# A convolution's magnitude sums on VectorE, a router that picks the first expert's rows itself, and two attentions in one stage

## The chip, the core and the metric

The kernel is one program on one core of a Trainium2 chip. It holds two transformer blocks in fp32. The metric is the device time of the whole program in microseconds (us); lower is better. The engines are named as in the profile: PE (TensorE matmul), PEld (its weight load), DVE (VectorE), ACT (ScalarE), POOL (GpSimd), SP (SyncE, which here only issues DMAs).

## The reference, cut to what matters

Three parts of the reference are touched. The first is the long convolution of the first block; o runs over its two orders:

```python
taps = jnp.concatenate([fwd, jnp.zeros_like(fwd[:1]), jnp.flip(bwd[1:], axis=0)], axis=0)
taps = taps / (jnp.sum(jnp.abs(taps), axis=0, keepdims=True) + EPS)
return jnp.fft.rfft(taps, axis=0)
...
for o, gate in enumerate((x1, x2)):
    zf = jnp.fft.rfft(z, n=2 * n, axis=1)
    conv = jnp.fft.irfft(zf * filt[None, :, o], n=2 * n, axis=1)[:, :n]
    z = gate * (conv + skip[o] * z)
```

The second is the mixture of 16 experts (4 groups of 4, the best two experts of one group for each of 512 tokens):

```python
scores = jax.nn.sigmoid((ht @ router_w).astype(f32))
sel = scores + router_b.astype(f32)
group_score = lax.top_k(sel.reshape(-1, N_GROUPS, EXPERTS_PER_GROUP), TOP_K)[0].sum(-1)
group = jnp.argmax(group_score, axis=-1)
_, idx = lax.top_k(jnp.where(in_group, sel, -jnp.inf), TOP_K)
for e in range(N_EXPERTS):
    hid = jax.nn.silu(ht @ w_gate[e]) * (ht @ w_up[e])
    out = out + gates[:, e:e + 1] * (hid @ w_down[e])
```

The third is two attentions of the second block that don't depend on one another. The dilated one has three groups of four heads (head size 64) that are merged by a softmax over their log-sums; the memory one has four heads (size 128) of 512 queries against 256 memory rows:

```python
alpha = jax.nn.softmax(jnp.stack(lses, axis=0), axis=0)
o_dil = jnp.sum(alpha[..., None] * jnp.stack(outs, axis=0), axis=0)
...
sm = jnp.einsum('bqhc,bkhc->bhqk', qm, kv[:, :, 0]) * (MEM_HEAD_DIM ** -0.5)
pm = jax.nn.softmax(sm, axis=-1)
om = jnp.einsum('bhqk,bkhc->bqhc', pm, kv[:, :, 1]).reshape(B, S, MEM_WIDTH)
```

## The kernel before, in words

The program is a row of stages. Each is one `nc.Block()`, in which every engine has its own written-out list of instructions, and semaphores order them across engines; all engines meet at the end of a stage. PSUM has 8 banks of 128x512, `K.ps`. A matmul whose operands are plain fp32 stands in the profile as two records. The large weight products are written as three matmuls with operands split into a rounded high part and a rest: ACT makes the high part of a weight chunk (`high`), DVE or POOL subtracts to get the low part (`low`).

Weights come through a ring (`Ring`, L49) of four slots of 1 MB. SP issues load k once `used` has reached k - 3, and that count grows when a chunk's slot has been read; in the expert stage DVE's `low` does it.

**Long convolution** (`hyena_stage`, L1671). For each order o, four token phases i: PE makes the filter values (`filters`), ACT the decay window, DVE multiplies them and makes the sum and difference (`tap_pair`), ACT takes their magnitudes (`magnitude`), and PE adds the magnitudes up over the tokens by multiplying with ones (`sums`, L1735, two matmuls for each of the four phases). DVE adds the skip term to the first row (`patch`). PE transforms signal (`"z"`) and filter (`"f"`), each in two halves j of four groups D, B, A, C (`group`, two matmuls of 128x512 each). ACT evicts D and B, DVE adds and subtracts A and C (`add`). DVE multiplies the spectra (`products`, seven operations of up to 128x2048), corrects one row (`row_products`, `row_again`), and PE transforms back (`inverse`) into the four banks `B_OUT`, from where DVE multiplies with the gate. The banks `B_OUT` are those of D, B, A and C, and so `inverse` waits until `add` of the last filter half has read them.

**Router** (`router_stage`, L2272). ACT and DVE finish the norm, PE multiplies with the router's matrix and transposes the hidden tokens into rows `K.h_rows`. DVE ranks the 4 groups and the 4 experts in each group by pairwise comparisons, one after another, each waiting for the one before (`then`, `tt`, L2378). `masked` lets PE count each token's place in its expert's list. From the places DVE works out the slot numbers (`K.put`, `keyed`), and POOL scatters the token rows into `h_slots` in DRAM with eight indirect DMAs. Behind that DVE makes the weights, the overflow list, the rates of the later recurrence (`le` to `K.lru_rate`) and the norm of the memory rows (`m_rec`, `m_root`, eight scalings of `K.memT`). SP stores `gate_rows` and waits until they have landed.

**Experts** (`moe_stage`, L2485). For expert e, SP reads its 128 rows from `h_slots`, PE transposes them (`turn_rows`), ACT and DVE split them (`high_rows`, `low_rows`), and PE multiplies with six weight chunks: `hidden(e)` takes four, `down(e)` two, each chunk 12 matmuls of 128x512. Parts of four chunks fit in SBUF; `high(c)` waits until chunk c - 4 has been used. The stage reads 96 chunks.

**Second block's attentions.** `dilated_attention_stage` (L3183) takes 12 batches through scores, bias and maximum, exponential, transpose, and values. Then a tail merges the groups: DVE alone works through rows of 4x512 (two maxima, three differences, three products, two sums, a reciprocal, three products) with one exponential for each group on ACT, PE spreads the three results over 128 partitions (6 matmuls, L3289), and DVE multiplies and adds (L3383, L3387). Only then `memory_attention_stage` (L3391) begins, which calls `attention_stage` (L1356): 16 steps of scores, maximum, exponential, division (L1455), transpose and copy, and every fourth step the values of one head. The merge stage follows.

## Time and profile before

| | us |
|---|---|
| median of 3 runs | 2403.51 |
| lowest and highest of them | 2399.74, 2410.54 |
| time of the profiled execution | 2399.45 |
| its span, first to last instruction | 2397.6 |

So 1.85 us of the profiled execution lie around the span, and it is 4.06 us under the median of the runs. Busy shares of the span are PE 91%, PEld 68%, DVE 47%, ACT 36% and POOL 22%. The mean granted clock of TensorE is 0.943 of full speed. A row of the timeline gives the start, the busy time, engine, line and operation, how many instructions it merges, and in brackets how long the engine sat idle before it and what released it. A row of windows gives the stretch, its length, the busy time of each engine with its instructions, the granted clock, the DMA share and GB/s.

### The profile page before, as it was taken

The numbers are of one execution on the slowest core, as the hardware profiler recorded it, in microseconds if no ns is written. First come the engines' busy times: TensorE is split into PE (matmuls) and PEld (weight loads), VectorE is DVE, ScalarE is ACT, GpSimd is POOL, SyncE is SP. The second block draws the span as 40 slices with busy tenths as digits, with TensorE's granted clock in tenths as the row PEclk, the third lists the DMA queues.
The fourth block names the chain that finished last, engine by engine and source line by source line (L and its number), as shares of the span: only waits on it lengthen the run. The fifth ranks groups of instructions, "written<-read, shape, count | busy, mean of one in ns | idle before, by whom it ended". The sixth has DMA issues, their size and how long they took to land. (4 is left out here: it accounts for less than half of the span.)

```text
span 2397.6 us, 23687 instructions
## 1 busy us (share of the span) xinstructions
PE 2178.0 (91%) x9454; PEld 1633.3 (68%) x9454; DVE 1128.6 (47%) x1471; ACT 870.5 (36%) x1123; POOL 537.4 (22%) x165
## 2 busy tenths in 40 slices
PE   6999999999879999859999969899699988999997
PEld 3767855574348887748777747687378876887885
DVE  3453356734662234278888556405622245223223
ACT  4532223333113223247777536515332232211221
POOL 1320210130004444010000003430044442443440
PEclk9995999999989999879999989999799999999999
DMA  6241224321014232259999932221022233222210
GB/s 233 88 151 63 81 71 141 106 92 44 0 36 132 79 97 100 67 216 356 385 385 389 329 120 88 92 88 45 0 80 88 88 106 105 90 104 87 87 53 35
DMA packets 174846, 299.68 MB, mean 125 GB/s; under 512 B 8943, under 2 KB 66490, under 8 KB 174744
## 3 DMA queue, kind: packets, MB, share of 16 engines
q1 hardware_dynamic: 169400, 279.93, 33.6%
q0 software_dynamic: 3040, 9.93, 1.2%
q10 hardware_dynamic: 2304, 8.39, 0.9%
q8 instruction: 72, 1.18, 0.2%
q14 instruction: 30, 0.25, 0.0%
HBM read 275.10 MB, written 23.13 MB: 124 GB/s over the span
## 5 line engine op out<-in xcount | busy, mean ns | idle before, releaser
L130 POOL TENSOR_TENSOR region<-weights,region 128x2048 fp32r<-128x2048 f32 (+2 forms) x94 | 366.5, 3901 | 1057.9 <-ACT region L124 769.6
L240 PE MATMUL ps<-region 128*128 128x512 f32 (+1 forms) x1336 | 535.0, 400 | 41.7 <-DVE region L2228 11.8
L243 PE MATMUL ps<-region 128*128 128x512 f32 (+1 forms) x1336 | 520.4, 389 | 0.0
L244 PE MATMUL ps<-region 128*128 128x512 f32 (+1 forms) x1336 | 519.9, 389 | 0.0
L240 PEld LDWEIGHTS ps<-region 128*128 128x128 f32 x1336 | 259.2, 194 | 108.2 <-issue 22.3
L243 PEld LDWEIGHTS ps<-region 128*128 128x128 f32 x1336 | 259.4, 194 | 54.6 <-issue 6.5
L244 PEld LDWEIGHTS ps<-region 128*128 128x128 f32 x1336 | 258.9, 194 | 50.8
L124 ACT ACTIVATE region<-weights 128x2048 fp32r<-128x2048 f32 (+2 forms) x98 | 158.5, 1621 | 295.9 <-PE ps L244 245.0
L2716 DVE TENSOR_TENSOR region<-weights,region 128x2048 fp32r<-128x2048 f32 x96 | 218.7, 2290 | 52.5 <-ACT region L2639 52.4
L2639 ACT ACTIVATE region<-weights 128x2048 fp32r<-128x2048 f32 x96 | 183.8, 1918 | 69.5 <-DMA weights<-moe_w_up 29.8
L281 PE MATMUL ps<-region 128*128 128x512 f32 x480 | 192.0, 400 | 6.7 <-DVE region L3583 4.1
L3424 POOL TENSOR_TENSOR region<-weights,region 128x2048 fp32r<-128x2048 f32 x30 | 143.0, 4780 | 226.1 <-ACT region L3536 178.3
L283 PE MATMUL ps<-region 128*128 128x512 f32 x480 | 187.1, 390 | 0.0
L282 PE MATMUL ps<-region 128*128 128x512 f32 x480 | 186.8, 389 | 0.0
L2555 PE MATMUL ps<-region 128*128 128x512 f32 x384 | 154.9, 403 | 10.7 <-issue 8.7
L2246 DVE TENSOR_TENSOR region<-ps,region 128x512 f32<-128x512 f32 x48 | 33.1, 690 | 259.6 <-PE ps L244 259.6
L2556 PE MATMUL ps<-region 128*128 128x512 f32 x384 | 152.0, 396 | 0.0
L2557 PE MATMUL ps<-region 128*128 128x512 f32 x384 | 151.7, 395 | 0.0
L281 PEld LDWEIGHTS ps<-region 128*128 128x128 f32 x480 | 90.2, 188 | 29.9 <-DVE region L3587 6.0
L3591 DVE TENSOR_TENSOR region<-ps,region 128x512 f32<-128x512 f32 x64 | 44.3, 692 | 128.7 <-PE ps L283 128.7
L3536 ACT ACTIVATE region<-weights 128x2048 fp32r<-128x2048 f32 x32 | 60.3, 1911 | 122.1 <-PE ps L3512 118.2
L283 PEld LDWEIGHTS ps<-region 128*128 128x128 f32 x480 | 90.1, 188 | 19.1
(396 smaller groups left out, 2810.4 us busy)
## 6 DMA issues: line engine op xcount, KB each, us to landing
weights<-w_in SPq DMA_DIRECT2D x54, 1024.0 KB, 5.1
weights<-moe_w_gate SPq DMA_DIRECT2D x32, 1024.0 KB, 7.7
weights<-moe_w_up SPq DMA_DIRECT2D x32, 1024.0 KB, 8.7
weights<-moe_w_down SPq DMA_DIRECT2D x32, 1024.0 KB, 7.6
weights<-w_mod SPq DMA_DIRECT2D x24, 1024.0 KB, 5.1
weights<-w_mlp_in SPq DMA_DIRECT2D x16, 1024.0 KB, 5.2
weights<-w_mlp_out SPq DMA_DIRECT2D x16, 1024.0 KB, 5.0
h_slots<-region SPq DMA_DIRECT2D x16, 512.0 KB
```

What stands on the lines that cost most here:

```text
L124: act.activation(flat(self.part(K, n, 0)), flat(r.view(n)), ACT.Copy).then_inc(self.hi_done, 1)
L130: eng.tensor_tensor(flat(self.part(K, n, 1)), flat(self.ring.view(n)), flat(self.part(K, n, 0)).bitcast(F32), ALU.subtract).then_inc(self. ...
L240: ins = pe.matmul(out, l_hi, r_hi, start=(start and k == 0), stop=False)
L243: pe.matmul(out, l_hi, r_lo, start=False, stop=False)
L244: ins = pe.matmul(out, l_lo, r_hi, start=False, stop=(stop and k == kt - 1))
L281: pe.matmul(out, w_hi, x_hi, start=(n == 0), stop=False)
L282: pe.matmul(out, w_hi, x_lo, start=False, stop=False)
L283: last = pe.matmul(out, w_lo, x_hi, start=False, stop=(n == len(triples) - 1))
L2555: pe.matmul(K.ps[:, bank, :], x_hi[:, x, :], w_hi[:, k, :], start=(start and k == 0), stop=False)
L2556: pe.matmul(K.ps[:, bank, :], x_hi[:, x, :], w_lo[:, k, :], start=False, stop=False)
L2639: act.activation(flat(part(c, 0)), r.slots[n % RING][:, :], ACT.Copy).then_inc(hi_done, 1)
L2716: dve.tensor_tensor(flat(part(c, 1)), r.slots[n % RING][:, :], flat(part(c, 0)).bitcast(F32), ALU.subtract).then_inc(r.used, 1)
```

## The change

In the convolution, DVE adds the magnitudes of the four phases into `prod` (`sizes`, three adds for each order), and PE sums only that, with two matmuls for each order in place of eight. The inverse transform writes into the banks of the sums and the edge, D and B, and no longer waits for the last `add`. The filter's A and C groups start with the half that needs no patch (`patched_taps`). The orders of all three engines' lists are changed, and DVE's last `products` is cut into two halves of columns, which the last inverse follows.

```diff
-    B_OUT = (B_D, B_B, B_A, B_C)
+    B_OUT = (B_SUM, B_EDGE, B_D, B_B)
...
+            def sums(o):
+                pe.wait_ge(size_done, 3 * o + 3)
+                if o:
+                    pe.wait_ge(out_done, 4)
+                for t in range(2):
+                    ins = pe.matmul(K.ps[0:1, B_SUM, :], K.ones[:, 0:1], prod[:, t, :], start=(t == 0), stop=(t == 1))
                 ins.then_inc(sum_done, 1)
...
+                if kind == "f" and j == 0 and not odd:
+
+                    pe.matmul(K.ps[:, bank, :], *pairs[1], start=True, stop=False)
+                    return pairs[0]
                 accumulate(pe, K.ps[:, bank, :], pairs).then_inc(tr, 1)
+
+            def patched_taps(o):
+
+                rest = [group("f", o, 0, part) for part in "AC"]
+                pe.wait_ge(patched, 4 * o + 4)
+                for (w, x), bank in zip(rest, (B_A, B_C)):
+                    pe.matmul(K.ps[:, bank, :], w, x, start=False, stop=True).then_inc(tr, 1)
...
                 if j == 0:
                     q = q_of("f", o, 1)
                     pe.wait_ge(fixed, 2 * o + 2)
+                    pe.wait_ge(rows, 2 * o + 2)
+                    pe.wait_ge(scaled, 1 if o == 0 else 2)
                     pe.wait_ge(ev_d, reads_of_d[q + 1])
                     pe.wait_ge(ev_b, q + 1)
-                    pe.wait_ge(added, 2 * q + 2)
                 G = four(Z, j)
                 for m in range(4):
+                    if o and j and m == 2:
+                        pe.wait_ge(step, 35)
                     if o == 0:
...
             filters(0, 1)
             groups("z", 0, 0, "AC")
             filters(0, 2)
-            sums(0, 0)
             groups("z", 0, 1, "DB")
             filters(0, 3)
-            sums(0, 1)
             groups("z", 0, 1, "AC")
-            sums(0, 2)
-            sums(0, 3)
-            groups("f", 0, 0, "DBAC")
+            groups("f", 0, 0, "DB")
+            sums(0)
+            patched_taps(0)
             edge(0)
             columns(0)
+            groups("f", 0, 1, "DBAC")
             filters(1, 0)
...
-            sums(1, 1)
             inverse(0, 1)
+            filters(1, 1)
+            groups("z", 1, 0, "DB")
...
+            groups("z", 1, 1, "DBAC")
+            groups("f", 1, 0, "DB")
+            sums(1)
+            patched_taps(1)
...
+            def sizes(o, i):
+
+                dve.wait_ge(abs_done, 4 * o + i + 1)
+                if i > 1:
+                    dve.wait_ge(size_done, 3 * o + i - 1)
+                dve.tensor_tensor(prod[:, 0:2, :], pair_of(o, 0) if i == 1 else prod[:, 0:2, :], pair_of(o, i), ALU.add)                    .then_inc(size_done, 1)
...
+            def products(o, j, half=None):
+
+
+                c = slice(0, S) if half is None else slice(256 * half, 256 * half + 256)
+                z, f, p = four(Z, j)[:, :, c], four(F, j)[:, :, c], prod[:, :, c]
+                n = 14 * o + 7 * j + (7 if half else 0)
...
             add("z", 0, 0)
+            sizes(0, 1)
             tap_pair(0, 2)
             tap_pair(0, 3)
+            sizes(0, 2)
+            sizes(0, 3)
+            add("z", 0, 1)
             patch(0)
-            add("z", 0, 1)
             add("f", 0, 0)
             scale(0)
+            row_products(0)
             products(0, 0)
-            row_products(0)
             row_again(0)
-            tap_pair(1, 0)
             add("f", 0, 1)
             products(0, 1)
-            tap_pair(1, 1)
+            tap_pair(1, 0)
             for m in range(4):
                 dve.wait_ge(inv_done, m + 1)
                 dve.tensor_tensor(K.x1[:, m, :], K.ps[:, B_OUT[m], :], K.x1[:, m, :], ALU.mult).then_inc(out_done, 1)
...
-            products(1, 1)
+            products(1, 1, 0)
+            products(1, 1, 1)
```

In the router, the groups' scores are ranked with the experts' in one array of 80 columns, three widths at a time. PE counts places with 5 matmuls in place of 14. A one-hot matrix `hot` lets PE pick the first expert's 128 rows, already transposed, from `K.h_rows`, and ACT and DVE split them; ACT and DVE also split the first four weight chunks, and SP issues the next four loads before it stores `gate_rows`. The recurrence's rates are made at the start of the stage; the memory rows' norm goes to the expert stage (DVE in experts 2 and 4, ACT in expert 3). The expert stage starts with `hidden(0)` at once.

```diff
+EARLY = 4
...
+            r.issue_until(sp, n0 + EARLY + RING)
             sp.wait_ge(copied, 1)
             sp.dma_start(K.gate_rows, oT).then_inc(stored, 16)
...
+            pe.wait_ge(masked, 1)
+            pe.matmul(K.ps[:, 1, 0:80], upto, mask, start=True, stop=False)
+            for b in range(ST):
+                later = mask[:, b * NEXP:(b + 1) * NEXP].unsqueeze(1).broadcast_to([P, ST - b, NEXP])
+                ins = pe.matmul(K.ps[:, 1, (b + 1) * NEXP:80].rearrange("p (t e) -> p t e", e=NEXP), K.ones[:, :], later,
+                                start=False, stop=(b == ST - 1))
+            ins.then_inc(place_done, 1)
...
+            pe.wait_ge(rows_done, 2 * ST)
+            pe.wait_ge(hot_done, 1)
+            for half in range(2):
+                for c in range(4):
+                    k = 4 * half + c
+                    ins = accumulate(pe, K.ps[:, 3 + half, c * P:(c + 1) * P],
+                                     [(K.h_rows[:, t, k * P:(k + 1) * P], hot[:, t, :]) for t in range(ST)])
+                ins.then_inc(picked, 1)
...
+            for c in range(EARLY):
+                act.wait_ge(r.arrived[(n0 + c) % RING], r.arrival(n0 + c))
+                act.activation(flat(expert_weights(K, c, 0)), r.slots[(n0 + c) % RING][:, :], ACT.Copy).then_inc(weights_hi, 1)
...
+            first_high(0)
             act.wait_ge(s_done, 2)
             act.activation(oT, K.ps[0:NEXP, 6, :], ACT.Copy).then_inc(copied, 1)
-            act.wait_ge(decayed, 1)
...
+            first_high(1)
...
+            weights_low(0)
+            weights_low(1)
             dve.wait_ge(sig_done, 1)
...
+            tt(both_sel[:, 64:80], t1, t2, ALU.add)
+
+            v4, r4 = e4(both_sel), e4(both_rank)
+            for d in range(1, 4):
+                w = gt[:, 0:20 * (4 - d)].rearrange("p (g e) -> p g e", e=4 - d)
+                tt(w, v4[:, :, d:4], v4[:, :, 0:4 - d], ALU.is_gt)
+                tt(r4[:, :, 0:4 - d], r4[:, :, 0:4 - d], w, ALU.add)
+                then(dve.scalar_tensor_tensor(r4[:, :, d:4], r4[:, :, d:4], 1.0, w, ALU.add, ALU.subtract))
...
+            dve.tensor_tensor(hot, slot_no.unsqueeze(1).broadcast_to([P, ST, P]), chosen.broadcast_to([P, ST, P]),
+                              ALU.is_equal).then_inc(hot_done, 1)
...
+            weights_low(2)
+            weights_low(3)
...
+                if e == 3:
+                    act.wait_ge(mem_rec, 2)
+                    act.activation(m_root, m_rec, ACT.Sqrt).then_inc(mem_root, 1)
...
+                if e == 2:
+                    dve.tensor_scalar(m_rec, K.ps[:, 7, 0:NCTX], 1.0 / D, EPS, ALU.mult, ALU.add).then_inc(mem_rec, 1)
+                    dve.wait_ge(mem_rec, 1)
+                    dve.reciprocal(m_rec, m_rec).then_inc(mem_rec, 1)
+                if e == 4:
+                    dve.wait_ge(mem_root, 1)
+                    for k in range(KD):
+                        dve.scalar_tensor_tensor(K.memT[:, k, :], K.memT[:, k, :], K.vec("g_mem_2", k), m_root, ALU.mult,
+                                                 ALU.mult).then_inc(scaled, 1)
```

The two attentions share one stage: `second_attention_stage` runs the 12 dilated batches as its lead (`lead=True`), then the 16 steps of the memory attention, with the dilated tail dealt out beside them. The operations on rows of 4x512 are on POOL, save the two maxima (DVE, steps 2 and 3) and the reciprocal (DVE, step 11); PE spreads in steps 16 to 18, and DVE's four last multiplications and their adds stand at the end.

```diff
+    def dve(self, dve, a):
+        mrow = self.mrow
+        if a == 2:
...
+        if a == 11:
+            dve.wait_ge(self.summed, 2)
+            dve.reciprocal(self.m, self.m).then_inc(self.summed, 1)
+        if a == 17:
+            dve.wait_ge(self.o_copied, self.NB)
+            self.weigh_group(dve, 0)
+            self.weigh_group(dve, 1)
+
+    def pool(self, pool):
...
+        pool.wait_ge(chain, 2)
+        for g in range(3):
+            pool.tensor_tensor(mrow[:, g, :], mrow[:, g, :], m, ALU.subtract).then_inc(chain, 1)
+        for g in range(3):
+            pool.wait_ge(self.e_done, g + 1)
+            pool.wait_ge(chain, 5 + g)
...
+        pool.tensor_tensor(t0, drow[:, 1, :], drow[:, 2, :], ALU.add).then_inc(summed, 1)
+        pool.wait_ge(summed, 1)
+        pool.tensor_tensor(m, m, t0, ALU.add).then_inc(summed, 1)
+        pool.wait_ge(summed, 3)
+        for g in range(3):
+            pool.tensor_tensor(drow[:, g, :], mrow[:, g, :], m, ALU.mult).then_inc(chain, 1)
```

## Rows read from the trace of the kernel before

**Rows 1.** Busy time by stretch: dilated tail, memory attention, long convolution, router, expert stage

```profile
1684.90:1709.10 24.20, 10.60 (x12) 3.62 (x12) 18.37 (x24) 1.85 (x4) 0.00 (x0) 0.51 0.00 0
1709.10:1741.60 32.50, 22.93 (x80) 12.43 (x80) 20.70 (x80) 11.43 (x36) 0.00 (x0) 0.89 0.00 1
...
563.00:713.20 150.20, 127.21 (x314) 54.22 (x314) 95.22 (x101) 33.76 (x43) 0.00 (x0) 0.93 0.04 13
1001.00:1048.50 47.50, 27.14 (x144) 25.62 (x144) 29.77 (x121) 16.47 (x24) 8.14 (x8) 0.61 0.30 112
...
1056.30:1358.50 302.20, 285.42 (x1312) 232.50 (x1312) 252.35 (x157) 226.03 (x188) 0.00 (x0) 0.99 1.01 374
```

**Rows 2.** Timeline of PE in the long convolution

```profile
588.88 3.59 PE L1739 MATMUL ps<-region,ones 128*1 128x512 f32 x8
...
618.93 3.78 PE L1731 MATMUL ps<-region 64*128 64x512 f32 x4 [5.85 <-DVE region L1946]
...
637.46 7.13 PE L1802 MATMUL ps<-region,weights 128*128 128x512 f32 x16
...
679.54 7.13 PE L263 MATMUL ps<-region,weights 128*128 128x512 f32 x16
695.82 8.72 PE L1807 MATMUL ps<-weights,region 128*128 128x256 f32 x32 [9.14 <-DVE region L1984]
```

**Rows 3.** Timeline of DVE in the long convolution

```profile
606.53 1.23 DVE L1994 TENSOR_TENSOR region<-region 128x1024 f32<-128x1024 f32 x1
...
693.34 1.20 DVE L1983 TENSOR_TENSOR region<-ps,region 128x1024 f32<-128x1024 f32 x1
```

**Rows 4.** Windows of 1 us in the long convolution; PEclk is the granted clock

```profile
689.00:690.00 1.00, 0.00 (x0) 0.00 (x0) 0.96 (x2) 0.00 (x0) 0.00 (x0) 0.50 0.00 0
...
699.00:700.00 1.00, 1.00 (x6) 0.90 (x5) 1.00 (x2) 0.00 (x0) 0.00 (x0) 0.99 1.07 369
```

**Rows 5.** Timeline of DVE in the router

```profile
1018.47 0.07 DVE L2397 MEMSET region<- 128x16 f32 x1
...
1026.79 0.23 DVE L2412 SCALAR_TENSOR_TENSOR region<-region 128x64 f32<-128x64 f32 x1
...
1033.11 0.17 DVE L2436 CAST slot_index<-region 128x8 int32<-128x8 f32 x1
...
1044.74 3.26 DVE L2476 SCALAR_TENSOR_TENSOR region<-region,vec_cols 128x256 f32<-128x256 f32 x8 [0.48 <-issue]
```

**Rows 6.** Timeline of PE from the router into the expert stage

```profile
1016.22 5.46 PE L2331 MATMUL ps<-ident,region 128*128 128x128 f32 x32
...
1056.28 0.76 PE L2555 MATMUL ps<-region 128*128 128x512 f32 x1 [2.06 <-ACT region L2644]
```

**Rows 7.** Timeline of POOL in the router: the last of eight scatters

```profile
1043.46 0.97 POOL L2306 DMA_INDIRECT h_slots<-region,slot_index  x1 [0.30 <-issue]
```

**Rows 8.** Expert stage: DMA queue's waits; its DMA total; issues on SP; page's landing time

```profile
SPq L87 <- DVE region L2716: 258.7, 95, 6.2
...
DMA packets 53843, 113.79 MB, mean 374 GB/s; under 512 B 1952, under 2 KB 1952, under 8 KB 53828
...
1066.10 3.26 SPq L87 DMA_DIRECT2D weights<-moe_w_down  x2
...
weights<-moe_w_up SPq DMA_DIRECT2D x32, 1024.0 KB, 8.7
```

**Rows 9.** Timeline of DVE in the dilated tail and memory attention

```profile
1691.61 3.34 DVE L3374 RECIPROCAL region<-region 4x512 f32<-4x512 f32 x1
...
1710.81 0.42 DVE L1442 TENSOR_REDUCE region<-ps 128x1 f32<-128x256 f32 x1 [1.76 <-PE ps L1393]
...
1738.42 0.42 DVE L1463 COPY region<-ps 128x256 f32<-128x256 f32 x1 [0.59 <-PE ps L1403]
```

**Rows 10.** POOL's groups by form; the durations of one DVE line (L3046)

```profile
L130 POOL TENSOR_TENSOR region<-weights,region 128x512 fp32r<-128x512 f32 x6 | 8.1, 1359 | 61.3 <-ACT region L124 61.3
...
L3046 DVE TENSOR_SCALAR region<-region x6: 426/428/1769, 1463.1 to 1521.6; 128x512 f32<-128x512 f32 x6
```

More of the change, by code:

```diff
@@ L1370, in _ @@
         def _(pool):
+            if lead:
+                beside.pool(pool)
             for n in first:
@@ L1387, in _ @@
         def _(pe):
+            if lead:
+                beside.lead_pe(pe)
             for a in range(NB + 3):
@@ L1415, in _ @@
         def _(act):
+            if lead:
+                beside.lead_act(act)
             for a in range(NB + 3):
@@ L1436, in _ @@
         def _(dve):
+            if lead:
+                beside.lead_dve(dve)
             for a in range(NB + 2):
@@ L1463, in _ @@
                     dve.tensor_copy(PT[:, h % 2, :, (b % ST) * P:(b % ST + 1) * P], tbank()).then_inc(copied, 1)
+            if lead:
+                beside.last_dve(dve)
 def latent_attention_stage(K):
@@ L1857, in _ @@
             inverse(1, 1)
-            pe.matmul(K.ps[:, B_EDGE, 0:1], K.ones[:, :], K.ones[:, 0:1], start=True, stop=True).then_inc(r.used, 1)
+            pe.matmul(K.ps[:, B_A, 0:1], K.ones[:, :], K.ones[:, 0:1], start=True, stop=True).then_inc(r.used, 1)
         @block.scalar
@@ L2051, in _ @@
                 dve.tensor_tensor(K.x1[:, m, :], K.ps[:, B_OUT[m], :], K.x1[:, m, :], ALU.mult).then_inc(out_done, 1)
+            tap_pair(1, 1)
+            sizes(1, 1)
             tap_pair(1, 2)
@@ L2054, in _ @@
             tap_pair(1, 3)
+            sizes(1, 2)
+            sizes(1, 3)
+            add("z", 1, 1)
             patch(1)
-            add("z", 1, 1)
             add("f", 1, 0)
@@ new lines, in _ @@
+            for b in range(ST):
[11 more added lines that the diff above has]
+                ins.then_inc(picked, 1)
+                if half == 0:
+                    pe.wait_ge(over_done, 1)
+                    for t in range(ST):
+                        ins = pe.transpose(K.ps[0:NEXP, 6, t * P:(t + 1) * P], over[:, t * NEXP:(t + 1) * NEXP],
+                                           K.ident[:, :])
+                    ins.then_inc(s_done, 1)
@@ L2728, in low_hidden @@
                                   ALU.subtract).then_inc(ht_lo_done, 1)
-            for c in range(3):
-                low(c)
-                if c == 0:
-                    low_rows(0)
             for e in range(NEXP):
@@ L3391, in memory_attention_stage, with probs, sums, scores @@
-def memory_attention_stage(K):
+    def probs(self, b):
+        n = P * self.blocks[b]
+        return self.Pb[:, b % 3, 0:self.HEADS * n].rearrange("p (a k) -> p a k", k=n)
+    def sums(self, b, i):
+        return self.stats[:, i, b * self.HEADS:(b + 1) * self.HEADS].rearrange("p (r a) -> p a r", a=2)
+    def scores(self, pe, b):
+        K = self.K
+        g, j = self.batches[b]
+        n = P * self.blocks[b]
+        if b >= 2:
+            pe.wait_ge(self.biased, b - 1)
+        for h in range(self.HEADS):
+            c, rows = g * 2 + h // 2, slice(64 * (h % 2), 64 * (h % 2) + 64)
+            out = K.ps[:, 2 * (b % 2) + h % 2, (h // 2) * n:(h // 2 + 1) * n]
+            ins = pe.matmul(out, group_tokens(K.qd[rows, c, :], g, j), self.key_view(g, j, rows, c), start=True, stop=True)
+        ins.then_inc(self.s_done, 1)
@@ new lines, in lead_pe, with pe @@
+    def lead_pe(self, pe):
+        NB = self.NB
+        for a in range(NB + 3):
+            if a < NB:
+                self.scores(pe, a)
+            if 0 <= a - 2 < NB:
+                self.turn(pe, a - 2)
+            if a >= 3:
+                self.values(pe, a - 3)
+    def pe(self, pe, a):
+        if a == 2:
+            pe.wait_ge(self.o_copied, self.NB)
+            pe.wait_ge(self.st_copied, 2 * self.NB)
+        if a >= 16:
+            self.spread(pe, 2 * (a - 16))
+            self.spread(pe, 2 * (a - 16) + 1)
@@ new lines, in spread, with weigh @@
+    def spread(self, pe, i):
+        K = self.K
+        if i % 2 == 0:
+            pe.wait_ge(self.chain, 8 + i // 2 + 1)
+        if i >= 4:
+            pe.wait_ge(self.part, i - 3)
+        pe.matmul(K.ps[:, 2 * (i % 4) + 1, :], K.pick[:, (i % 2) * P:(i % 2 + 1) * P], self.drow[:, i // 2, :],
+                  start=True, stop=True).then_inc(self.bc_done, 1)
+    def weigh(self, act, b):
+        act.wait_ge(self.neg_done, 2 * (b + 1))
+        for h in range(self.HEADS):
+            c = b * self.HEADS + h
+            p = self.probs(b)[:, self.at(h), :]
+            act.activation(p, p, ACT.Exp, bias=self.stats[:, 1, c:c + 1], accum_out=self.stats[:, 2, c:c + 1])\
+                .then_inc(self.exp_done, 1)
```

524 lines of the change are left out of this document (223 added, 301 removed).

## The prediction

> **What bounds the kernel now.** First the busy shares of the page: PE 91%, so time is won where PE waits or does work that can go. Then the windows of busy time: PE's idle time lies in few places. The long convolution takes 150.2 us with PE busy for 127.2; the router 47.5 with 27.1; between router and the first expert matmul lie 7.8 more; the dilated tail takes 24.2 with 10.6, most of it at a granted clock of 0.51; the memory attention 32.5 with 22.9 [rows 1]. The expert stage is another case: 302.2 us, PE busy for 285.4, the DMA engines at a share of 1.01 [rows 1]. Its SP waited 258.7 us in 95 waits, all for DVE's `low` [rows 8], so a load is issued when a slot is free and never earlier. Last come the timelines of PE and DVE in these stretches. All times below are on the clock of the profiled execution; "new" times are worked out on it with each stage's start held where it was.
>
> **The convolution.** Four ones-matmuls took 3.59 us, 0.9 each [rows 2]. Sixteen become four: 10.8 us less on PE. DVE gets six adds of 128x1024 at 1.23 [rows 3], 7.4 us; it is busy for 95.2 of 150.2 us [rows 1], and I let idle time hide them. If that cover were gone they would cost 7.4.
>
> I walked the new lists engine by engine, with 0.9 us for a 512-column matmul and the timeline's DVE durations (0.69 for 128x512, 1.23 for 128x1024, 2.28 for 128x2048).
> - Order 0: PE no longer meets the sums of phases 0 to 3 (7.2 us); one pair (1.8) returns behind the filter's D and B, where PE would next wait for the patch. Half of A and C is done before the patch. The first `products` starts at 601.8 instead of 604.2, the second follows without `tap_pair(1, 0)` between (2.7 us), and ends at 624.4. The second inverse of order 0 then starts at 624.5. Before it was 637.46 [rows 2], behind two sums of order 1 that waited for ACT's magnitudes. 13.0 us earlier.
> - Order 1 up to the last filter half: PE does three `filters` (5.7), 24 group matmuls (21.8), the sums and the edge (3.6), the inverse (7.2), and waits some 2 us (gate, patch). 624.5 + 40.5 gives 665.0 for the start of the last filter groups, before 679.54 [rows 2]: 14.5 earlier.
> - The end: DVE's row products and first `products` end at 678.9 with the corrected row, and the inverse begins there, no longer behind `add` (693.34 and the next, 2.3 us [rows 3]): 695.82 [rows 2] becomes 678.9, 16.9 earlier. The inverse takes 8.7 as before. The halves of the last `products` cost 5.2 each, 10.4 instead of 9.5, and end at 686.4 and 691.6, so the last two columns of the inverse begin at 691.7, and the last of DVE ends at 696.1, before 713.2 [rows 1]: 17.1.
> - The clock: PE will idle for 4.7 us ahead of the first inverse, 4 ahead of the second, 6.7 ahead of the third. In the trace it fell to 0.50 in PE's idle stretch behind 686.7 and was back at 699, some 3 us after work began at 695.82 [rows 2, 4]; filters that take 1.9 took 3.78 behind the earlier idle stretch [rows 2]. The second inverse is on the path and would lose 0 to 3.6 us; I take 1.
> Gain 16, from 12 to 18.
>
> **Router and experts.** The norm starts 0.9 us later (five small DVE operations ahead of it). Ranking took from 1018.47 to 1026.79, 8.3 us in 39 operations [rows 5]; nine of about 0.25 make 2.2. `masked` comes at 1022.0 instead of 1027.1. PE's transposes (5.46 [rows 6]) end at 1022.6 and are what is late next; 5 matmuls count places by 1023.9; the slot numbers are cast at 1027.2 instead of 1033.11 [rows 5]. POOL's scatters end 5.9 us earlier, at 1038.5 [rows 7]. PE's picking is 64 records of 128x128 at 0.12 to 0.21 (full clock, half clock), 7.7 to 13.6 us from 1025.0, and the memory sums 3.6 more: 1036.8 to 1043. DVE ends at 1037.2: it has lost the memory norm (3.26 [rows 5], and the reciprocal) and gained two `low` of 2.3 ahead of the lists. So engines alone end the stage at 1038.5.
>
> One added wait is behind that: SP now issues loads 6 and 7 (free at 1029.7 and 1032.0) ahead of `gate_rows`, and the stage waits for its landing. Both loads and the scatters, 6.3 MB, at the 374 GB/s of the expert stage [rows 8] take 17 us from 1028: at worst 1045. Between 1038.5 and 1045 I take 1042: `gate_rows` needs only the two loads ahead of it, not all scatters, to be through.
> [...]
>
> `hidden(0)` then starts at about 1042.7 instead of 1056.28 [rows 6]: 13.6. Does that reach the end of the stage? The end is set by 96 chunks that pass four slots, each waiting for landing (8.7 us, [rows 8]), ACT and DVE. Load 8 was issued at 1066.10 [rows 8]; now it needs the first chunk used (12 matmuls at half clock, 5.1 us: 1047.8) and split (1.9 and 2.3): 1052.2. 13.9 earlier, with loads 4 to 7 long landed. From there on the stream is as before, save 5.5 us of memory norm on DVE in experts 2 and 4 and an exchange of tables on ACT (about 3 us), of which DVE's slack of 50 us in 302 [rows 1] hides most; uncovered it costs 5.5. Gain 14, from 8 to 18.
>
> **The attentions.** The lead ends as before at 1684.9. The memory loop took from 1710.81 to 1738.42 and the end of its copy, 28.0 us [rows 9], 1.31 a step with DVE as its bound and stalls of 1.4 at every head. It can begin at 1684.6: end at 1712.6. Added on DVE: two maxima (1.4), the reciprocal 3.34 [rows 9] less a stall of 1.4 that it covers, two multiplications in step 17 (1.4), a stall behind PE's spreads (1.2), then four multiplications with adds (5.8): 1724.3 instead of 1741.6 [rows 1], 17.3 less. [...]
>
> New is POOL beside DVE. A POOL operation on 512 columns took 1359 ns [rows 10] (on 128 partitions; four partitions bound it from above), 11 of them 15 us. A DVE operation from SBUF to SBUF that takes 426 ns took up to 1769, both long ones next to a POOL operation, and ended with it [rows 10]. Each step has one such operation of 256 columns (the division). At worst every POOL operation holds DVE once for its whole length: 15 us, at best nothing. Steps and POOL operations are of one length, so a hold falls in somewhere; I take 0.4 us on each, 4.4. The chain itself (summed at step 11) comes within 1 us of its use. Gain 13, from 4 to 18.
> [...]
>
> **The sum.** 16 + 14 + 13 = 43. The profiled execution took 2399.45, so 2356.5; the median of the runs is 4.1 above it, which would make 2360.5. I predict 2358.
>
> **Rivals.**
> 1. Port held (chance 0.15): POOL and DVE hold each other for the whole 15 us, the attentions gain 13 + 4.4 - 15 = 2.4, the total is 32: 2369. For it: the 1769 ns. Against: of a step's operations only the division has more than one column on both sides in SBUF.
> 2. Head start lost (0.12): the expert stream isn't shifted whole, since DVE's and ACT's extra work and the landing of the second half set the pace, or `gate_rows` lands last; the 8.5 us of moved work come off the 14, router and experts gain 5.5, the total is 34.5: 2366. For it: a DMA share of 1.01. Against: the stream has no other start than load 8.
> 3. The change doesn't do what it says in the convolution (0.08): DVE, with 7.4 us of adds and halves, is the bound where PE was, and its 7.4 and 0.9 more come off the 16; the total is 35: 2366. For it: DVE is at 95.2 and runs unbroken for long stretches. Against: the adds stand before the transforms' results are there.
> 4. More than forecast (0.10): all three at their upper ends, 54: 2347.
> 5. Slower (0.03): the four slots of the ring are a loop, about 12.6 us for four chunks; were landing to take longer than 8.7 us because loads now meet rows and stores in another phase, each of 24 turns would cost the excess. From 43 / 24 = 1.8 us more the gain is gone, and at 3 us more (11.7) the kernel takes 2358 + 72 = 2430. Only the share of 1.01 speaks for it; against it, the stream's bytes and order are the same.
> The rest, 0.52, is the forecast as it stands.
>
> **Numbers.** What 0.5% is, 12 us, is about what a measurement can tell from no change. For "within" two of the first three rivals must come at their full size: 0.03. Faster 0.94, same 0.03, slower 0.03. The range has to take in the rivals singly and the first with a second, and the spread of the median (2399.7 to 2410.5): 2341 to 2379.
>
> **What would show it.** Right: six adds of 1.22 behind the magnitudes and the inverse of order 0 near 624 and 632 on the stage's clock; DVE's cast of the slots 5 to 6 us earlier; `hidden(0)` with no read of `h_slots` before it, some 13 us earlier from the router's start; load 8 before the end of `hidden(0)`; no stretch of DVE on 4x512 rows with PE idle, and 11 POOL rows. Wrong: the convolution's second half with DVE busy and PE waiting for `sizes`; the expert stage longer than 302.2 us by what the router won; divisions of over 1 us.

## The result and the profile after the change

| | before | after |
|---|---|---|
| median of 4 runs, us | 2403.73 | 2369.65 |
| lowest and highest | 2399.74, 2410.54 | 2365.38, 2373.5 |
| profiled execution, and its span | 2399.45, 2397.6 | 2370.18, 2368.4 |

The ratio of the times is 0.9855 with a 95% interval of 0.9827 to 0.9883: 35 us won, between 28 and 42, where 43 were summed up and 2358 was predicted. A second series of the same kernel, further down, gave 0.9841 (0.9816 to 0.9867), 38 us. One of the six executions of `e_load8` took 7981.15 us and stands outside its ratio. `e_before_nodrain`, `e_dve_rows` and `e_thin` have one execution each (2411.6, 2372.87 and 2341.8 us) and are read by their stages alone. Busy shares of the kernel after are PE 92%, PEld 69%, DVE 48%, ACT 37%, POOL 23%, and the mean clock is 0.946.

First the windows of the changed stretches in the kernel after: convolution, router up to DVE's end, router up to the first expert matmul, experts, joint attentions (columns as in [rows 1]).

```profile
568.05:705.80 137.75, 120.83 (x290) 54.71 (x290) 103.23 (x114) 33.35 (x43) 0.00 (x0) 0.90 0.04 14
993.30:1029.40 36.10, 32.27 (x190) 31.37 (x190) 30.23 (x91) 23.54 (x28) 7.09 (x5) 0.70 0.42 136
993.30:1041.70 48.40, 32.27 (x190) 31.39 (x191) 30.23 (x91) 23.54 (x28) 10.01 (x8) 0.68 0.55 197
1041.70:1344.90 303.20, 286.32 (x1309) 231.73 (x1309) 247.53 (x163) 223.13 (x186) 0.00 (x0) 0.99 0.99 360
1665.20:1708.80 43.60, 33.29 (x109) 16.25 (x109) 33.69 (x93) 14.75 (x48) 13.95 (x11) 0.83 0.00 1
```

Against [rows 1] the convolution takes 137.75 instead of 150.2, and the two attentions 43.6 from DVE's last copy in the lead to DVE's last operation. The router is the surprise. Its engines are through 36.1 us after the stage's start, but the first expert matmul comes at 48.4: 12.3 us in which PE does nothing. The timelines of SP, POOL and PE there:

```profile
1022.21 2.57 SPq L87 DMA_DIRECT2D weights<-moe_w_up  x2
1024.82 0.69 SPq L2362 DMA_DIRECT2D gate_rows<-region  x1
...
1020.80 2.35 POOL L2352 DMA_INDIRECT h_slots<-region,slot_index  x1 [65.12 <-DVE slot_index L2526]
1023.46 1.82 POOL L2352 DMA_INDIRECT h_slots<-region,slot_index  x1 [0.30 <-issue]
...
1031.97 0.97 POOL L2352 DMA_INDIRECT h_slots<-region,slot_index  x1 [0.30 <-issue]
...
1041.71 0.76 PE L2627 MATMUL ps<-region 128*128 128x512 f32 x1 [12.48 <-PEq L2345]
```

And SP's own waits in the router (line waited for; total, times, longest; `SPq` and `PEq` are the engines' sequencers, which wait and issue):

```profile
SPq L2345 <- DMA gate_rows<-region: 10.5, 1, 10.5
SPq L2345 <- PEq L2345: 5.4, 1, 5.4
```

L2345 is the router's block. SP had issued `gate_rows` by 1025.5 and waited 10.5 for its landing, to 1036.0. Then it stood 5.4 more at the end of the block, at which DVE, ACT and PE had been since 1029.4 and POOL's last instruction since 1032.9. The windows of the DMA engines say what was still going on:

```profile
1026.00:1028.00 2.00, 2.00 (x11) 1.74 (x11) 1.79 (x8) 0.41 (x1) 1.52 (x2) 1.00 1.01 316
1034.00:1036.00 2.00, 0.00 (x0) 0.00 (x0) 0.00 (x0) 0.00 (x0) 0.00 (x0) 0.50 1.05 421
1038.00:1040.00 2.00, 0.00 (x0) 0.00 (x0) 0.00 (x0) 0.00 (x0) 0.00 (x0) 0.50 1.02 420
1040.00:1042.00 2.00, 0.29 (x1) 0.32 (x2) 0.00 (x0) 0.00 (x0) 0.00 (x0) 0.50 0.18 74
```

They were full until about 1040.3, with two loads and eight scatters (6.34 MB in the windows from 1022 to 1042), and the stage ended a microsecond behind the last of it. The two loads (2.1 MB, the second asked for at 1024.4) and the store were through at 1036.0, some 12 us behind that second request, where 420 GB/s alone would have moved them in 5: they shared the engines with the scatters, whose queue moved 2.37 MB before 1036 and 1.83 MB behind it.

One profile alone would mislead about the rest. The table has the length of each changed stretch in the profiled execution of every kernel below. "Router" is from the start of the norm on DVE, which has 0.9 us of new work in front of it, to the first `hidden` matmul; "to expert end" from the same start to the last matmul of the expert stage; "attentions" from DVE's last copy in the lead to the first DVE operation of the stage behind.

| kernel | convolution | router | to expert end | attentions |
|---|---|---|---|---|
| before | 150.1 | 55.3 | 401.5 | 61.6 |
| after | 137.7 | 47.5 | 396.1 | 47.8 |
| after, again (`e_same`) | 132.4 | 47.7 | 396.2 | 47.8 |
| `e_conv` | 132.4 | 55.2 | 410.3 | 63.1 |
| `e_router` | 150.1 | 46.6 | 401.7 | 63.1 |
| `e_attn` | 150.1 | 55.2 | 406.8 | 48.0 |
| `e_gate` | 132.4 | 49.0 | 397.2 | 47.8 |
| `e_nodrain` | 132.4 | 41.6 | 393.8 | 48.0 |
| `e_gate_nodrain` | 132.4 | 34.9 | 390.3 | 48.4 |
| `e_load8` | 137.7 | 35.9 | 391.9 | 48.1 |
| `e_dve_rows` | 132.4 | 46.9 | 399.5 | 55.7 |
| `e_before_nodrain` | 153.2 | 55.2 | 403.9 | 63.6 |
| `e_thin` | 132.4 | 46.5 | 375.7 | 47.8 |

### The profile page after: what moved, and what is told of

Same layout as the page of the kernel before. It is cut to its first block and busy times, and to the rows that moved or that the text cites. A ratio compares the mean times of both kernels' runs of the same rounds, so it can differ in the third digit from the quotient of the medians.

```text
span 2368.4 us, 23692 instructions
## 1 busy us (share of the span) xinstructions
PE 2178.0 (92%) x9468; PEld 1638.1 (69%) x9468; DVE 1125.5 (48%) x1447; ACT 871.6 (37%) x1124; POOL 552.9 (23%) x176
## 5 line engine op out<-in xcount | busy, mean ns | idle before, releaser
L240 PEld LDWEIGHTS ps<-region 128*128 128x128 f32 x1336 | 260.1, 195 | 109.0 <-issue 22.6
L243 PEld LDWEIGHTS ps<-region 128*128 128x128 f32 x1336 | 260.1, 195 | 55.0 <-issue 6.5
L244 PEld LDWEIGHTS ps<-region 128*128 128x128 f32 x1336 | 259.3, 194 | 50.8
L2788 DVE TENSOR_TENSOR region<-weights,region 128x2048 fp32r<-128x2048 f32 x92 | 209.4, 2288 | 67.9 <-ACT region L2712 67.8
L2712 ACT ACTIVATE region<-weights 128x2048 fp32r<-128x2048 f32 x92 | 176.2, 1918 | 86.9 <-DMA weights<-moe_w_up 30.8
L281 PEld LDWEIGHTS ps<-region 128*128 128x128 f32 x480 | 90.2, 188 | 29.9 <-DVE region L3693 6.0
L3642 ACT ACTIVATE region<-weights 128x2048 fp32r<-128x2048 f32 x32 | 60.3, 1910 | 122.0 <-PE ps L3618 118.1
L2627 PEld LDWEIGHTS ps<-region 128*128 128x128 f32 x384 | 73.0, 190 | 43.9 <-issue 26.0
```

What stands on the lines that cost most here:

```text
L240: ins = pe.matmul(out, l_hi, r_hi, start=(start and k == 0), stop=False)
L243: pe.matmul(out, l_hi, r_lo, start=False, stop=False)
L244: ins = pe.matmul(out, l_lo, r_hi, start=False, stop=(stop and k == kt - 1))
L281: pe.matmul(out, w_hi, x_hi, start=(n == 0), stop=False)
L2627: pe.matmul(K.ps[:, bank, :], x_hi[:, x, :], w_hi[:, k, :], start=(start and k == 0), stop=False)
L2712: act.activation(flat(part(c, 0)), r.slots[n % RING][:, :], ACT.Copy).then_inc(hi_done, 1)
```

## The experiments

### One part of the change at a time

`e_conv`, `e_router` and `e_attn` are the kernel before with the functions of one part replaced by those of the kernel after.

> The kernel before with the convolution's part of the change alone. The prediction gave this part 16 us (2387), the two traces show 12.4 (2391): PE's first filter to DVE's last operation took 150.1 before and 137.7 after, with the first filters and two of three inverses partly at half clock. If the slow clock at the stage's start is a matter of the single execution, this run's stage takes 134 to 135; if the change itself causes it, it takes 137 to 138. Nothing outside the stage should change its length.

Measured: 0.9936 of the time before (0.9914 to 0.9959), that is 15 us won, from 10 to 21. The stage took 132.4, below the 134 to 135 of the expectation's first reading, and so it did in seven of the nine executions with the new convolution. Timeline of PE in `e_conv`:

```profile
563.55 1.96 PE L1731 MATMUL ps<-region 64*128 64x512 f32 x4 [1.10 <-PEq L1505]
...
613.15 9.27 PE L1813 MATMUL ps<-region,weights 128*128 128x512 f32 x16 [4.82 <-issue]
624.77 7.13 PE L1813 MATMUL ps<-region,weights 128*128 128x512 f32 x16 [2.35 <-DVE region L2015]
...
664.72 7.13 PE L263 MATMUL ps<-region,weights 128*128 128x512 f32 x16
678.69 12.41 PE L1818 MATMUL ps<-weights,region 128*128 128x256 f32 x48 [6.83 <-issue]
691.46 3.72 PE L1818 MATMUL ps<-weights,region 128*128 128x256 f32 x16 [0.36 <-DVE region L2015]
```

In the profile of the kernel after the same lines are slower:

```profile
632.43 8.83 PE L1823 MATMUL ps<-region,weights 128*128 128x512 f32 x16 [2.10 <-DVE region L2025]
...
688.04 16.96 PE L1828 MATMUL ps<-weights,region 128*128 128x256 f32 x64 [6.83 <-issue]
```

A window at the start of its stage:

```profile
568.00:569.00 1.00, 0.92 (x1) 0.49 (x2) 0.00 (x0) 0.95 (x1) 0.00 (x0) 0.50 0.00 0
```

There the granted clock was 0.50 when the stage began, at 568.1 instead of 563.6, and the second inverse took 8.83 where it takes 7.13. The slow start cost 3.1 us, the second inverse 1.7 and the third 0.5. The three executions that reached this stage at 567.8 to 568.2 (after, `e_load8`, `e_before_nodrain`) had the convolution 5.3, 5.3 and 3.1 us longer than the others of the same code, which reached it at 559.4 to 564.1. So some 10 of the 43 us expected were missing from the one profile of the kernel after, 5 ahead of the stage and 5.3 in it; `e_before_nodrain`, with the old convolution, came late and slow in the same way, so the change isn't the reason. What sets an execution back like this, no run here shows.

> The kernel after the change once more, beside the run above on one chip. Its profile before had the convolution at 137.7 us where five other executions of the same code had 132.4, and its expert stage (first expert matmul to the stage's last) at 348.6 where others had 348 to 355. Expected here: convolution 132.4, router 46.5 to 49 from the norm's start to the first expert matmul, the joint attention stage 47.8 to 48.4, and 2365 to 2371 in all.

Measured: all as expected in the stages (132.4, 47.7, 47.8), and 2364.0, a little below the range given; the ratio is 0.9841.

> The kernel before with the attentions' part of the change alone. The prediction gave it 13 us (2390); in the traces the stretch from the lead's last copy to the next stage's first operation on DVE took 61.6 before and 47.8 after, 13.8 less. Here the same within 1 us, with 5 of 16 divisions longer than 0.35 us and 2 us of excess in all. Rival: POOL and DVE share badly and the excess comes to more than 4 us in another execution.

Measured: 0.9952 (0.9929 to 0.9976), 12 us won, from 6 to 17. The stretch took 48.0; the four executions with the old attentions had 61.6 to 63.6, mean 62.8.

> The kernel before with the router's and experts' part of the change alone. The prediction gave it 14 us (2390). From the traces: the router's start to the first expert matmul takes 48.4 instead of 55.3, 6.9 less, and of this and the early work 4.4 to 5.6 are left where the expert stage ends: 2398. The second reading is that the expert stage gives some of the head start back; if it is DMA's rate that takes it, the distance from load 8 to the last expert's hidden product is longer than before's by 3 to 5 us with the DMA engines' share above 1.0 throughout.

Measured: 0.9981 (0.9964 to 0.9999), 5 us won, from 0 to 9. The router took 46.6, and the end of the expert stage came at 401.7, inside what executions of the old code show (401.5, 410.3, 406.8, 403.9; mean 405.6). The five runs of the new code with the old stage's end (after, `e_same`, `e_gate`, `e_router`, `e_dve_rows`) have a mean of 398.1. Single executions of one kind lie up to 9 us apart, so these means are good to some 2 or 3 us, an estimate from that spread. The second reading of the expectation, an expert stage longer by 3 to 5 us, falls: from the first expert matmul to its end the stage took 346.2 to 355.2 with the old code and 348.2 to 355.1 with the new, 350.5 and 350.6 in the mean.

### What the router's end waits for

```diff
-            r.issue_until(sp, n0 + EARLY + RING)
+            r.issue_until(sp, n0 + 2 + RING)
             sp.wait_ge(copied, 1)
             sp.dma_start(K.gate_rows, oT).then_inc(stored, 16)
+            r.issue_until(sp, n0 + EARLY + RING)
             sp.wait_ge(stored, 16)
```

> The kernel after the change with one difference: in the router SP issues the store of the gate rows ahead of loads 6 and 7 instead of behind them. Theory: the router stage ended 8 us after the last engine because this store had to get through behind 2.1 MB of loads, interleaved with the scatters. With it ahead, the store lands some 2 to 3 us after about 1023 us on the trace's clock, and the stage ends with POOL's last scatter: the first expert matmul starts about 41 us after DVE's first operation of the router instead of 48.4, load 8 about 7 us earlier, the DMA engines' pause between the two is filled, and the kernel gains 6 to 8 us over the changed one (about 2363). Rival 1: the stage waits for the scatters' data themselves, not for the store: the first expert matmul stays at 48 and nothing is gained. Rival 2: the first matmul moves by 7, but the expert stream is held by the DMA engines' rate, so that at the end of the expert stage less than 3 us is left.

Measured: 0.9863 (0.9824 to 0.9901), no better than the kernel after. Rival 1 came true. SP's waits in the router of `e_gate`:

```profile
SPq L2345 <- PEq L2345: 18.6, 1, 18.6
...
SPq L2345 <- DMA gate_rows<-region: 0.5, 1, 0.5
```

The store was there at once, and then SP waited 18.6 us at the end of the block. Some 7 of them had passed when POOL's last instruction ended. The other 11 lie behind it, with no engine at work and the DMA engines full until some 3 us before the first expert matmul (a share of 0.92 even from 1030 to 1032, and the matmul at 1034.6). In `e_same`, whose trace has the landing of each scatter, the last one landed 47.1 us after the norm's start, and the first expert matmul came at 47.7. No semaphore of the router waits for them; the expert stage has its own wait. What remains is the end of the block itself. The next kernel takes the drain of GpSimd out of it; the expert stage's wait for the scatters still stands ahead of its read of the rows:

```diff
 def router_stage(K):
...
-    with K.nc.Block() as block:
+    with K.nc.Block(no_gpsimd_drain=True) as block:
```

> The kernel after the change; the router's block ends without the drain of GpSimd, so that it no longer waits there for the data of POOL's scatters (the expert stage waits for them by semaphore before it reads a row). The store of the gate rows stays behind loads 6 and 7. In the run with the store moved ahead, SP had the store's landing 2.5 us after its issue and then stood at the stage's end, and the first expert matmul still came only after the last scatter's data. Theory (the drain holds the stage): here the stage ends with whichever is later, POOL's last scatter (38.7 us after the norm begins) or the store behind two loads (at most as long as the DMA engines are full, about 46). First expert matmul 40 to 46 us after the norm's start instead of 47.5. Rival (the landing of the rows themselves is what everybody waits for by semaphore): unchanged at 47 to 49.

Measured: 0.9834 (0.98 to 0.9868), 40 us; the times alone don't tell it from the kernel after. The first expert matmul comes at 41.6 instead of 47.5. SP's waits in `e_nodrain`:

```profile
SPq L2345 <- DMA gate_rows<-region: 10.8, 1, 10.8
SPq L2596 <- DMA h_slots<-region,slot_index: 4.2, 1, 4.2
SPq L2345 <- PEq L2345: 0.2, 1, 0.2
```

The 5.4 us at the block's end have become 0.2; the landing of the store (10.8) is now last, as the prediction had it. The scatters are still awaited, 4.2 us, but by SP alone and with PE at work.

> Both: the store of the gate rows ahead of loads 6 and 7, and no drain of GpSimd at the end of the router's block. Theory: the stage ends with POOL's last scatter instruction, the first expert matmul comes 38.5 to 39.5 us after the norm's start instead of 47.5, and the next load 8.9 us behind it while the scatters' data still move, so that the DMA engines' pause of some 9 us ahead of load 8 is gone. The kernel should be 7 to 9 us faster than the one after the change: about 2361 where that has 2370. Rival: the expert stage is held by the DMA engines' rate and was so from its first loads on, then at its end 3 us or less are left.

Measured: 0.9819 (0.979 to 0.9849), median 2357.35: 43 us, the lowest ratio here, though its interval overlaps those of the kernel after. The first matmul comes at 34.9, earlier than expected, since the block now ends with DVE and not with POOL's last instruction. Of 12.7 us at the start, 7.8 are left at the expert stage's end (390.3 against 398.1), as far as one execution can say: from first matmul to end it took 355.5, as long as the longest of the nine above. SP's waits in `e_gate_nodrain` show what held the loads:

```profile
SPq L2597 <- DMA h_slots<-region,slot_index: 13.6, 1, 13.6
...
SPq L87 <- DVE region L2789: 8.1, 1, 8.1
...
SPq L2345 <- DMA gate_rows<-region: 0.4, 1, 0.4
```

Load 8 is queued on SP behind the wait for the scatters. It was issued 49.3 us after the norm's start, in the kernel after 56.7. The next kernel issues it ahead of that wait:

```diff
+            r.issue_until(sp, n0 + 9)
             sp.wait_ge(K.loaded, K.loads(0))
             for e in range(NEXP):
+                if e == 1:
+                    r.issue_until(sp, n0 + 10)
```

> The run with the store ahead and no drain had its first expert matmul 34.9 us after the norm's start, but SP then stood 13.6 us before the scatters' landing with load 8 queued behind that wait, and the DMA engines fell to shares of 0.45 and 0.28 for 4 us. Here, on top of it, SP issues load 8 before it waits for the scatters, and load 9 before it asks for the rows of expert 2. Theory (the expert stage is held by the DMA engines' rate): the idle 2.5 us of the DMA engines are filled, the stage's end comes 1 to 3 us earlier from the norm's start than 390.3, about 2355 for the kernel where the one after the change has 2369. Rival: the rows of expert 1 land 2 to 3 us later behind load 8, PE stands longer before hidden(1), and nothing is won or 2 us are lost.

Measured: 0.9826 (0.9796 to 0.9857), the expert stage's end at 391.9. Load 8 went out at 43.2 and the rows of expert 1 at 50.7, 2.2 later than before. This is the rival: nothing won. Load 8 alone was 6.1 us earlier; load 11 went out at 61.3, in `e_gate_nodrain` at 59.1, in `e_nodrain` at 61.2 and in the kernel after at 67.1. The ends of the expert stage (391.9, 390.3, 393.8, 396.1) go with load 11 and not with load 8, within what single executions can tell.

> The kernel before, with the router's block ending without the drain of GpSimd. There the expert stage begins with the rows that the scatters write, and DVE is busy to the stage's end, when the scatters' data have landed: the first expert matmul should stay at 55.2 us after the norm's start, within 1 us. If the drain itself costs time beyond the landing, it comes earlier by that much.

Measured: 55.2, as expected, where the table has 55.3 with the drain. The drain cost nothing here; in the kernel after, whose expert stage no longer begins with the scattered rows, it cost 5.9 (47.5 against 41.6).

### What holds the expert stage

`e_thin` leaves out a quarter of each weight chunk from load 8 on and multiplies old data in its place; only its times are read.

```diff
-            sp.dma_start(self.view(k), self.plan[k][1]).then_inc(self.arrived[k % RING], 16)
+            part = slice(0, 3 if self.plan[k][0] == "moe" and k >= self.first("moe") + 8 else None)
+            sp.dma_start(self.view(k)[:, part], self.plan[k][1][:, part]).then_inc(self.arrived[k % RING], 16)
```

> The kernel after the change, but each chunk load of the expert stage from load 8 on brings only three quarters of its bytes (one of four row blocks is left out and old data are multiplied in its place), with all engines' work unchanged. It asks whether the expert stage is held by the DMA engines (share 1.03, 375 to 385 GB/s) or by PE. If by DMA: the stage gets shorter down to what PE needs, 16 times 18.0 us of matmuls and transposes and the tail behind them, that is by 12 to 20 us, and PE's idle time in it goes. If by the loop over the four slots (ACT's and DVE's splitting, the landing time) or by PE: it gets shorter by less than 5 us.

Measured: 375.7 instead of 398.1, 22 us less and a little more than the 12 to 20 expected; the five executions behind the 398.1 lie between 396.1 and 401.7. A window of 40 us in the middle of the stage, first of the kernel after, then of `e_thin`:

```profile
1185.00:1225.00 40.00, 37.88 (x181) 30.93 (x180) 33.71 (x22) 29.52 (x26) 0.00 (x0) 1.00 1.04 383
```

```profile
1182.00:1222.00 40.00, 40.00 (x190) 33.28 (x189) 36.53 (x24) 32.65 (x28) 0.00 (x0) 1.00 0.93 335
```

With a quarter of the bytes gone PE no longer idles. The stage is held on the side of the loads, not by PE, ACT or DVE, whose work is the same. That it is the DMA engines' rate is the likeliest reading, for their share was 1.04. This run alone doesn't show it: a smaller load also lands sooner (median of the `moe_w_down` loads 5.2 us instead of 7.1), and landing is a part of the loop over the four slots too.

### POOL beside DVE

`e_dve_rows` gives the eleven operations to DVE, for example:

```diff
+        if 4 <= a < 7:
+            g = a - 4
+            if g == 0:
+                dve.wait_ge(chain, 2)
+            dve.tensor_tensor(mrow[:, g, :], mrow[:, g, :], m, ALU.subtract).then_inc(chain, 1)
```

> The kernel after the change, with the eleven operations on rows of 4x512 on DVE at steps 4 to 6, 8 to 10, 11, 12 and 13 to 15 of the joint stage instead of on POOL. It prices POOL's help against what it costs DVE. DVE takes on 11 operations at 0.63 to 0.68, 7.2 us, and loses the 2.0 us by which five divisions were longer than 0.35, and the wait of 0.9 for POOL's sum: the stretch from the lead's last copy to the next stage's first operation becomes 47.8 + 4.3 = 52 us, all divisions last 0.35. By rival 1 of the prediction (the two hold each other for POOL's whole 14 us) it would not be longer than 47.8 at all.

Measured: 55.7, where 52 was expected, so POOL's help is worth 7.9 us and not 4.3. All divisions last 0.35; the two stretches differ also by PE, for which DVE waits 2.6, 2.0 and 2.6 at the heads here, and 1.6, 1.4 and 1.3 in the kernel after. The lines of the kernel after, POOL and then DVE beside it:

```profile
1671.68 3.84 POOL L3462 TENSOR_TENSOR region<-region 4x512 f32<-4x512 f32 x3 [55.84 <-DVE region L3447]
...
1681.21 2.66 POOL L3469 TENSOR_TENSOR region<-region 4x512 f32<-4x512 f32 x2 [1.73 <-ACT region L3406]
...
1672.23 0.86 DVE L1463 TENSOR_SCALAR region<-region 128x256 f32<-128x256 f32 x1
...
1681.44 1.19 DVE L1463 TENSOR_SCALAR region<-region 128x256 f32<-128x256 f32 x1
...
1686.57 3.34 DVE L3450 RECIPROCAL region<-region 4x512 f32<-4x512 f32 x1 [0.88 <-POOL region L3473]
```

Five divisions of sixteen were longer than 0.35, by 2.0 us in all, in each of the eight executions with POOL in the stage (2.01 to 2.03); POOL was busy for 14.1.

## Why the prediction was right, and where not

The time lies in the range of 2341 to 2379, 12 us above the 2358 named. The sum came out right for the convolution, right by luck for the attentions, where two errors nearly cancel, and 7 too high for the router and the experts. The 35 us measured are also the totals of rivals 2 and 3 (34.5 and 35), but the runs show the mechanism of neither.

**Convolution: right, 17.7 instead of 16.** Set against `e_conv`, which began 0.45 us later, the walk through the lists was off by less than 1 us everywhere: second inverse 624.5 (measured 624.3), last filter groups 665.0 (664.3), third inverse 678.9 (678.2), end 696.1 (695.5). The adds cost nothing. The 1 us for the clock wasn't due in seven of nine executions: the clock did fall in the idle stretch ahead of the first and third inverse (in `e_conv` to 0.50 from 611 to 613 and to 0.59 from 675 to 678; the first took 9.27 us instead of 7.13), but DVE's `products` were last behind both. In the profile of the kernel after, and in `e_load8`, the second inverse did lose 1.7, as the forecast feared. Rival 3 is refuted: DVE does run unbroken there, and the stage's end is DVE's, but with the whole gain.

**Router: the engines right, the end wrong.** Counted from the stage's start, `masked` came at 21.0 (forecast 21.0), the cast of the slots at 26.5 (26.2), DVE's end at 36.1 (36.2). PE's picking took 7.6, at full clock (1.00 from 1017 to 1025). The scatters ended at 39.7, 2.2 later than forecast: their first two took 2.35 and 1.82 beside DVE's `low`, which had moved next to them. `gate_rows` landed at 42.7 and the sum had 41.0, and without the drain the first matmul came at 42.5, as forecast (41.7). The step that failed is "So engines alone end the stage at 1038.5", with one added wait behind it. There was a second, in no list: the end of the router's block waited for POOL's transfers, 5.4 us. Before the change it was hidden, since DVE was busy to 1048.0 and the next stage began with the scattered rows (in `e_before_nodrain` their last data landed 46.7 us after the norm's start and DVE ended at 47.0); the forecast took that need away and didn't ask what else stood behind the scatters. Of 13.6 us 6.9 came (48.4 instead of 55.3). Rival 2 named the size (5.5 for router and experts; 6.6 were left at the expert stage's end, by means of four and five executions) but the wrong cause: half of the head start wasn't lost in the stream, it had not been there. Of the prediction's own signs, "some 13 us earlier from the router's start" for `hidden(0)` is the one that failed here. Load 8 went out 6.4 us late against the forecast; in `e_nodrain`, 51.7 us after the stage's start, it was where the forecast had it (51.2).

**Experts: what there was of a head start came through.** The sum followed load 8 and called DVE's slack the cover. The memory norm did stay hidden (means of 350.5 and 350.6 from first matmul to end), but `e_thin`, 22 us shorter with a quarter of the bytes gone, shows that the stage waits for its loads: a head start counts only as far as it moves them. In `e_gate_nodrain` 12.7 us at the first matmul became 7.8 at the end.

**Attentions: 14.9 by the means, 13.8 by the two profiles, forecast 13; two errors that nearly cancel.** The holds were 2.0 us instead of 4.4. The forecast set them all on the division. The profile of the kernel after agrees: none of its reductions and copies of 256 columns was longer than 0.42, as in `e_dve_rows` with nothing on POOL. Rival 1, 15 us, is refuted, though one of its signs, a division of over 1 us, did come once (1.19). Against that, the sum has no term for the clock in this stage, and it fell. Windows of the end of the stage in the kernel after:

```profile
1690.00:1700.00 10.00, 7.19 (x25) 3.61 (x26) 7.55 (x29) 3.42 (x11) 3.82 (x3) 1.00 0.00 0
1700.00:1709.00 9.00, 9.00 (x14) 3.00 (x12) 7.15 (x12) 0.00 (x0) 0.00 (x0) 0.55 0.01 3
```

And PE's last head in its timeline:

```profile
1706.17 3.78 PE L263 MATMUL ps<-region 128*128 128x512 f32 x4
```

The same four matmuls took 1.98 before, at 1738.90. Behind the spreads and at half clock (0.50 from 1703 to 1709) they end 1.2 us after DVE, and the stage ends with ACT's copy of them, 1.9 us after DVE. The sum had set DVE's last operation (1724.3) against the stage's end before (1741.6), so these 1.9 us were missing from it.

**The sum.** 17.7, 6.6 and 14.9 make 39.2, against 35 (28 to 42) and 38 (32 to 44) measured. A little is given back behind the joint stage, from which it took 655.1 to the end by the mean of nine executions and 653.9 by that of the four with the old attentions. The three parts alone gave 15, 5 and 12; their intervals (10 to 21, 0 to 9, 6 to 17) take in 17.7, 6.6 and 14.9. Rival 4 and rival 5 did not come.

## What to carry to other kernels

Before a stage's start is moved forward, list everything that its predecessor's end waits for, transfers that the block drains among them (POOL's scatters here, 5.4 us), and not only the waits that stand in the lists: what was hidden behind a need of the next stage becomes the wait when that need is taken away. Where a stage waits for its loads, count a head start by the loads that go out earlier, several of them and not the first alone, and not by the first matmul. And read a stage's length in several executions before explaining a few microseconds of it.

## What the runs showed that was not expected

- The end of the router's block waits for GpSimd's own transfers: 5.4 us in the kernel after, 11 with the store out of the way, 0.2 without the drain.
- The indirect DMA instruction on POOL takes 0.97 as a rule [rows 7] and 2.35 and 1.82 beside DVE's subtractions of 128x2048, in all nine executions of the new router. Each time it ended 0.97 and 0.89 us after the end of a subtraction, as if POOL had been held until then; no run moves the subtractions away to prove it.
- The expert stage varied from 346 to 356 us and the pause behind it between 6.0 and 10.5, whatever the kernel (`e_thin`'s stage apart). The new convolution had two lengths, 132.4 and 137.7, and the longer one went with a start some 5 us late.
- The clock fell to 0.55 while PE had been busy for 7.2 of the 10 us before (the last fence).
